# High and low parts of the hidden state as one moving operand of 512 columns in the first sweep over the experts

## The chip, the cores and the metric

The kernel runs on one core of a Trainium2 chip. The metric is the time of the whole program on the device, in microseconds, as the median of several runs. A change within 0.2% of it is about what a measurement of this kernel cannot tell from no change.

## The reference, cut to what matters

The program computes two transformer layers with a mixture of experts and then a third block, whose last part is this one (256 tokens, width 1024):

```
sc = einsum('bshcd,hckd->bshck', q, sub_keys)         # 8 heads x 2 sides x 128 keys
v1, i1 = top_k(sc[..., 0, :], 16);  v2, i2 = top_k(sc[..., 1, :], 16)
cand = v1[..., :, None] + v2[..., None, :]            # 16 x 16 pairs per head
top, pos = top_k(cand, 16);  idx = i1 * 128 + i2 at pos;  gate = softmax(top)
u   = expert_down[idx];  act  = gelu(einsum('bld,blhkd->blhk', h, u))
coef = gate * act
out = einsum('blhk,blhkd->bld', coef, expert_up[idx]) # added to the residual
```

There are 128 x 128 = 16384 experts, each a row of 1024 numbers in `expert_down` and one in `expert_up`. All arithmetic is float32.

## The kernel before, in words

The kernel is a chain of stages; each has its own program for every engine, and a barrier stands between two. The last part is peer_scores (scores of keys), peer_values, peer_grid (gates laid out over the experts) and peer_mix (second sweep, over `expert_up`). The change is in the first sweep, `peer_values`, and in where its operands lie.

The sweep computes the Gelu of h times **every** expert row, in 128 units of 128 experts, and does the search for the best keys and pairs beside it. The matrix engine takes float32 operands rounded to a format called fp32r, so each product of a and b is made of three: with a = high + low, high(a) high(b) + high(a) low(b) + low(a) high(b). For h the two parts are made once (`peer_scores`, L2573 and L2583). For a unit n of expert rows (512 KB, loaded into slot n % 6):

- **high(n)**, L2638, ScalarE: the rounded copy, 128 x 1024, into slot n % 3.
- **low(n)**, L2664, VectorE: row minus rounded row, written over the loaded row.
- **product(n)**, L2616, TensorE: eight blocks of 128 of the contraction, three matmuls each with 256 tokens as moving columns, all into one half of a PSUM bank, n % 3 (banks 0 to 2). The weights are a block of the rows, high twice and low once.
- **Gelu(n)**, L2653, ScalarE: from PSUM into the column block n of `pair_grid`.

Order by engine. ScalarE: high(0), high(1), high(2), and then for every n: wait for product(n), high(n+3), Gelu(n). VectorE: for every n low(n), then a piece of side work: for n below 40, four units of five have a **row search** (`rows`, `top16`: five operations on 128 scores, each waiting for the one before it); from 41 to 72 every second unit has a **pair search** (`pairs`: an addition and the same five on 256); 73 and 74 have `lift` and `places`; unit 76 has `norm`, which waits for ScalarE's Exp in unit 74 (`EXP_AT`); from 77 to 100 every second has one of **mark, take and gather** (one operation on 2048 each). TensorE: product(n) waits for low(n) and for Gelu(n-3), whose bank it takes; before unit 102 (`TURN_AT`) come six transposes, whose results ScalarE copies out in three (L2647 to L2649). SyncE loads unit n+6 when product(n) is done.

All waits are semaphores that count up: `high_made`, `low_made`, `summed` (a product is done), `gelued`, and so on.

Of the kernel before, what the change touches and what calls it, by code (L numbers as in the profile page):

```python
# [15 lines left out]
F32 = mybir.dt.float32  # L16
U32 = mybir.dt.uint32
I32 = mybir.dt.int32
F32R = mybir.dt.float32r
# [4 lines left out]
P = 128  # L24
T = 256
# [223 lines left out]
def half(ps, b):  # L249

    return ps[:, b // 2, (b % 2) * T:(b % 2) * T + T]
# [2224 lines left out]
class PeerMemory:  # L2476
# [3 lines left out]
    def __init__(self, k, ctx):  # L2480
        self.k = k
        grid_at = -(-k.nc.sbuf_base // 32) * 32
        self.qt = k.nc.alloc_sbuf_tensor_at("peer_q", [P, 2 * PH, T], F32, offset=grid_at + 48 * 1024)
        linear(k, "peer_queries", [("peer_query", 4, 0)], k.h, self.qt, ahead=0)
        self.grid = k.sb("pair_grid", [P, NK, T], ctx=ctx)
        self.lists = k.sb("peer_lists", [P, 2, T], ctx=ctx)
        self.i2_minus = k.sb("peer_second_list", [P, T], F32R, ctx=ctx)
        self.ident, self.ones, self.iota = (k.sb(f"peer_{n}", [P, P], F32R, ctx=ctx) for n in ("ident", "ones", "iota"))

        def units(name, first, n, dt, shape=None):  # L2490
            return k.nc.alloc_sbuf_tensor_at(name, shape or [P, n, D], dt, offset=k.ring_at + first * 4096)
        self.raw = units("expert_rows", 0, PEER_RAW, F32)
        self.low = units("expert_rows_low", 0, PEER_RAW, F32R)
        self.high = units("expert_rows_high", PEER_RAW, PEER_HIGH, F32R)
        self.h_high = units("peer_h_high", PEER_RAW + PEER_HIGH, 2, F32R, [P, KC, T])
        self.h_low = k.nc.alloc_sbuf_tensor_at("peer_h_low", [P, KC, T], F32R, offset=k.h_at)
        self.first = units("peer_first", PEER_RAW, 2, F32, [P, 4, QUAD, NK])
        self.second = units("peer_second", PEER_RAW + 2, 2, F32, [P, 4, QUAD, NK])
        self.apart = units("peer_apart", PEER_RAW + 4, 2, F32, [P, 4, QUAD * NK])
        self.coef_high = units("peer_coef_high", PEER_RAW + PEER_HIGH, 1, F32R, [P, 4, T])  # L2500
        self.coef_low = units("peer_coef_low", PEER_RAW + PEER_HIGH + 1, 1, F32R, [P, 4, T])
        self.rows = k.nc.alloc_sbuf_tensor_at("out_rows", [P, TT, D], F32, offset=k.h_at)

        self.at = grid_at + 64 * 1024
        self.kn = self.place("peer_keys", [P, 2 * PH, P])
        self.kt = self.place("peer_keysT", [P, 2 * PH, NK])
        self.sc = self.place("peer_scores", [P, TT, 2 * PH, NK])
        self.at = grid_at + 104 * 1024
        self.v = self.place("peer_best", [P, TT, 2 * PH, TOPK])
        self.ix = self.place("peer_best_ix", [P, TT, 2 * PH, TOPK], U32)  # L2510
        self.ixf = self.place("peer_best_ixf", [P, TT, 2 * PH, TOPK])
        self.top = self.place("peer_top", [P, TT, PH, TOPK])
        self.pos = self.place("peer_pos", [P, TT, PH, TOPK], U32)
        self.pa = self.place("peer_pos_a", [P, TT, PH, TOPK], U32)
        self.pf = self.place("peer_pos_f", [P, 2, TT, PH, TOPK])
        self.key = self.place("peer_key", [P, 2, TT, PH, TOPK])
        self.stat = self.place("peer_stat", [P, TT, PH])
        self.cand = self.place("peer_cand", [P, 2, TOPK, TOPK])
        self.hot = self.place("peer_hot", [P, PH, TOPK, TOPK])
        assert self.at <= grid_at + 128 * 1024  # L2520
# [17 lines left out]
def peer_scores(k, m):  # L2538

    H = PH  # L2540
    qt, kn, kt, sc = m.qt, m.kn, m.kt, m.sc
    with k.stage("peer_scores") as st:
        block = st.block
        in_keys, turned, moved, scored, scores_out, h_made, h_split = st.signals(7)

        @block.gpsimd
        def _(pool):
            st.clear_last(pool)

        @block.sync  # L2550
        def _(sp):
            sp.dma_start(kn[:], k.a["peer_sub_keys_2"][0].rearrange("h c k d -> k (h c) d")).then_inc(in_keys, 16)
            for n in range(PEER_RAW):
                m.load(sp, n)

        def four(b):
            return k.ps[:, b:b + 4, :].rearrange("p b (e t) -> p (b e) t", e=4)

        @block.tensor
        def _(pe):  # L2560
            pe.wait_ge(in_keys, 16)
            for n in range(2 * H):
                mm = pe.transpose(four(0)[:, n], kn[:, n], k.ident)
            mm.then_inc(turned, 1)
            pe.wait_ge(moved, 1)
            for i in range(TT):
                for n in range(2 * H):
                    mm = pe.matmul(four(4 * (1 - i))[:, n], qt[:, n, i * P:(i + 1) * P], kt[:, n], start=True, stop=True)
                mm.then_inc(scored, 1)

        @block.scalar
        def _(act):
            act.activation(m.h_high[:], k.h, ACT.Copy).then_inc(h_made, 1)  # L2573
            act.wait_ge(turned, 1)
            act.activation(kt[:], four(0), ACT.Copy).then_inc(moved, 1)
            for i in range(TT):
                act.wait_ge(scored, i + 1)
                act.activation(sc[:, i], four(4 * (1 - i)), ACT.Copy).then_inc(scores_out, 1)

        @block.vector  # L2580
        def _(dve):
            dve.wait_ge(h_made, 1)
            dve.tensor_tensor(m.h_low[:], k.h, m.h_high[:].bitcast(F32), ALU.subtract).then_inc(h_split, 1)  # L2583
            for dst, src in ((m.ident, k.ident), (m.ones, k.ones), (m.iota, k.iota)):
                dve.tensor_copy(dst[:], src).then_inc(h_split, 1)


def peer_values(k, m):
# [5 lines left out]
    SCORES_END, LATE = 96 - 16, 104  # L2594
    with k.stage("peer_values") as st:
        block = st.block
        high_made, low_made, summed, gelued, chain, ranked, apart, exped, normed, chosen, turned, moved = st.signals(12)

        @block.gpsimd
        def _(pool):  # L2600
# [8 lines left out]
        def product(pe, s, it):  # L2609
            n = it * PEER_RAW + s  # L2610
            pe.wait_ge(low_made, n + 1)
            pe.wait_ge(gelued, n + 1)
            for c in range(KC):
                hi, lo = m.high[:, s % PEER_HIGH, c * P:(c + 1) * P], m.low[:, s, c * P:(c + 1) * P]
                for q, (w, x) in enumerate(((hi, m.h_high), (hi, m.h_low), (lo, m.h_high))):
                    mm = pe.matmul(half(k.ps, 2 * (s % 3)), w, x[:, c], start=(c == 0 and q == 0), stop=(c == KC - 1 and q == 2))  # L2616
            mm.then_inc(summed, 1)

        @block.tensor
# [11 lines left out]

        @block.scalar
        def _(act):
            act.sem_inc(gelued, 3)

            def high(n):
                act.wait_ge(k.experts_in[n % PEER_RAW], loaded_units(n))
                act.activation(m.high[:, n % PEER_HIGH], m.raw[:, n % PEER_RAW], ACT.Copy).then_inc(high_made, 1)  # L2638

            for n in range(PEER_HIGH):  # L2640
                high(n)
            for n in range(NK):
                if n == SCORES_END:
                    act.wait_ge(ranked, 1)
                if n == TURN_AT:
                    act.wait_ge(turned, 1)
                    act.activation(m.lists[:, 0], half(k.ps, 8), ACT.Copy).then_inc(moved, 1)  # L2647
                    act.activation(m.lists[:, 1], half(k.ps, 10), ACT.Copy).then_inc(moved, 1)
                    act.activation(m.i2_minus[:], half(k.ps, 9), ACT.Copy, scale=-1.0).then_inc(moved, 1)  # L2649
                act.wait_ge(summed, n + 1)  # L2650
                if n + PEER_HIGH < NK:
                    high(n + PEER_HIGH)
                act.activation(m.grid[:, n:n + 1], half(k.ps, 2 * (n % 3)).unsqueeze(1), ACT.Gelu).then_inc(gelued, 1)  # L2653
                if n == EXP_AT:
                    act.wait_ge(apart, 1)
                    act.activation(top[:], top[:], ACT.Exp).then_inc(exped, 1)

        @block.vector
        def _(dve):
# [54 lines left out]
            def gather(n):  # L2714
                side, i = divmod(n, TT)
                dve.tensor_reduce(key[:, side, i].rearrange("p h r -> p (h r)"), f, AX.X, ALU.add).then_inc(chosen, 1)

            for n in range(NK):
                low(n)
                if n < 40 and n % 5 < 4:  # L2720
                    rows(n // 5 * 4 + n % 5)
                if n == 40:
# [5 lines left out]
                    lift()  # L2728
                if n == 74:
                    places()  # L2730
                if n == EXP_AT + 2:
                    norm()
                if 77 <= n < 101:
                    if (n - 77) % 6 == 0:
# [2 lines left out]
                        take((n - 77) // 6)  # L2737
                    if (n - 77) % 6 == 4:
                        gather((n - 77) // 6)


def peer_grid(k, m):
# [337 lines left out]
```

## Time and profile before

| | us |
|---|---|
| median of 3 runs | 4452.86 |
| lowest and highest run | 4451.96, 4454.59 |
| the profiled execution, whole | 4446.22 |
| its span in the profile | 4444.4 |
| TensorE busy in the span | 3906.9 (88%) |
| VectorE busy | 2328.8 (52%) |
| ScalarE busy | 1864.2 (42%) |

The profiled execution is one of its own, 6.64 us below the median of the three; 1.82 us of it lie outside the span. PE is TensorE's matmul, PEld its weight load, DVE VectorE, ACT ScalarE. The stage peer_values lies at 3499.3 to 3873.0 us of the span. In the timeline a matmul's record is longer than the distance to the next one's start: matmuls overlap, and what one costs in a row of them is read from the starts.

### The profile page before, as it was taken

Reading aid. Unit: us, or ns where it says so; the run is one execution under the profiler, and the core shown is the slowest. Engines: PE = TensorE matmul, PEld = TensorE weight load, DVE = VectorE, ACT = ScalarE, POOL = GpSimd, SP = SyncE. Lnnn points to the kernel's source line nnn. Section 1 sums busy time; section 2 is a strip of 40 time slices with the busy share of each in tenths; the row PEclk is TensorE's granted clock in tenths of the full one; section 3 lists DMA queues with packets and bytes.
Section 4 is the critical chain, followed back from the end, with each engine's and each line's share of the span. In section 5 each row is a group of like instructions: output and inputs, shape, how many; then the busy total and the mean of one; then the engine's idle time right before and its main releaser. Section 6 shows DMA issues by size and latency. Waiting matters only on the chain. (4 is left out here: it accounts for less than half of the span.)

```text
span 4444.4 us, 55601 instructions
## 1 busy us (share of the span) xinstructions
PE 3906.9 (88%) x21753; PEld 3255.8 (73%) x21753; DVE 2328.8 (52%) x2807; ACT 1864.2 (42%) x1955; POOL 54.5 (1%) x28
## 2 busy tenths in 40 slices
PE   6899878997948778999999996795687899999999
PEld 1792867997938656777777875795366899977887
DVE  0332632443346226888888872334423588455665
ACT  0333151333341416767767662343221344433554
POOL 0000000000000000000000000000000000000000
PEclk9999878998969779999999998897578999956999
DMA  7456003443500117999999982352003456501665
GB/s 237 160 190 227 5 1 114 170 151 133 190 23 1 38 57 265 361 363 361 363 363 361 363 317 85 114 183 74 6 15 119 127 184 180 161 1 35 193 193 165
DMA packets 308099, 738.78 MB, mean 166 GB/s; under 512 B 16154, under 2 KB 16609, under 8 KB 307937
## 3 DMA queue, kind: packets, MB, share of 16 engines
q1 hardware_dynamic: 307936, 736.60, 48.2%
q8 instruction: 105, 1.72, 0.2%
q14 instruction: 58, 0.47, 0.0%
HBM read 735.50 MB, written 1.05 MB: 166 GB/s over the span
## 5 line engine op out<-in xcount | busy, mean ns | idle before, releaser
L1777 DVE TENSOR_TENSOR weight_ring_low<-weight_ring,weights_high 128x2048 fp32r<-128x2048 f32 x336 | 772.8, 2341 | 148.9 <-ACT weights_high L1723 148.9
L1723 ACT ACTIVATE weights_high<-weight_ring 128x2048 fp32r<-128x2048 f32 x336 | 618.3, 1908 | 6.6 <-DMA weight_ring<-in_moe_w 6.6
L305 PE MATMUL psum_all<-h_high_projections,high_projections 128*128 128x256 f32 x1536 | 436.5, 284 | 50.0 <-DVE weight_ring_low L341 50.0
L305 PE MATMUL psum_all<-h_low_projections,high_projections 128*128 128x256 f32 x1536 | 436.2, 284 | 0.0
L305 PE MATMUL psum_all<-h_high_projections,weight_ring_low 128*128 128x256 f32 x1536 | 430.6, 280 | 0.0
L1665 PE MATMUL psum_all<-weights_high,expert_in_turn_high 128*128 128x512 f32 x896 | 359.3, 401 | 17.5 <-DVE weight_ring_low L1777 11.4
L341 DVE TENSOR_TENSOR weight_ring_low<-weight_ring,high_projections 128x2048 fp32r<-128x2048 f32 x96 | 215.4, 2288 | 303.3 <-ACT high_projections L327 303.3
L1665 PE MATMUL psum_all<-weights_high,expert_in_turn_low 128*128 128x512 f32 x896 | 356.2, 398 | 0.0
L1665 PE MATMUL psum_all<-weight_ring_low,expert_in_turn_high 128*128 128x512 f32 x896 | 351.7, 393 | 0.0
L305 PEld LDWEIGHTS psum_all<-h_high_projections,high_projections 128*128 128x128 f32 x1536 | 291.9, 190 | 51.2 <-issue 51.2
L305 PEld LDWEIGHTS psum_all<-h_high_projections,weight_ring_low 128*128 128x128 f32 x1536 | 296.1, 193 | 0.0
L2616 PE MATMUL psum_all<-peer_h_high,expert_rows_high 128*128 128x256 f32 x1024 | 291.1, 284 | 5.0 <-DVE expert_rows_low L2664 5.0
L305 PEld LDWEIGHTS psum_all<-h_low_projections,high_projections 128*128 128x128 f32 x1536 | 292.2, 190 | 0.0
L2616 PE MATMUL psum_all<-peer_h_low,expert_rows_high 128*128 128x256 f32 x1024 | 290.6, 284 | 0.0
L2616 PE MATMUL psum_all<-peer_h_high,expert_rows_low 128*128 128x256 f32 x1024 | 290.6, 284 | 0.0
L2638 ACT ACTIVATE expert_rows_high<-expert_rows 128x1024 fp32r<-128x1024 f32 x128 | 135.2, 1058 | 192.8 <-PE psum_all L2616 190.7
L1665 PEld LDWEIGHTS psum_all<-weights_high,expert_in_turn_high 128*128 128x128 f32 x896 | 168.7, 188 | 61.5 <-issue 20.5
L2664 DVE TENSOR_TENSOR expert_rows_low<-expert_rows,expert_rows_high 128x1024 fp32r<-128x1024 f32 x128 | 156.6, 1225 | 96.8 <-ACT expert_rows_high L2638 94.8
L2616 PEld LDWEIGHTS psum_all<-peer_h_high,expert_rows_high 128*128 128x128 f32 x1024 | 197.5, 193 | 5.4 <-DVE expert_rows_low L2664 5.4
L1665 PEld LDWEIGHTS psum_all<-weight_ring_low,expert_in_turn_high 128*128 128x128 f32 x896 | 168.4, 188 | 40.2
L2616 PEld LDWEIGHTS psum_all<-peer_h_low,expert_rows_high 128*128 128x128 f32 x1024 | 197.5, 193 | 0.0
L2616 PEld LDWEIGHTS psum_all<-peer_h_high,expert_rows_low 128*128 128x128 f32 x1024 | 197.4, 193 | 0.0
(563 smaller groups left out, 7811.7 us busy)
## 6 DMA issues: line engine op xcount, KB each, us to landing
weight_ring<-in_moe_w SPq DMA_DIRECT2D x336, 1024.0 KB, 5.2
weight_ring<-in_w_in SPq DMA_DIRECT2D x48, 2048.0 KB, 8.5
expert_rows<-in_peer_down SPq DMA_DIRECT2D x128, 512.0 KB, 3.6
expert_rows<-in_peer_up SPq DMA_DIRECT2D x128, 512.0 KB, 3.6
weight_ring<-in_ada_w SPq DMA_DIRECT2D x24, 2048.0 KB, 8.0
weight_ring<-in_ffn_w SPq DMA_DIRECT2D x21, 2048.0 KB, 7.8
weight_ring<-in_w_out SPq DMA_DIRECT2D x6, 2048.0 KB, 8.1
weight_ring<-in_w_up_dn SPq DMA_DIRECT2D x4, 2048.0 KB, 8.0
```

The lines of the kernel that those rows point to most:

```text
L305: mm = pe.matmul(half(k.ps, 4 * (g % R) + j), w[:, c, j * P:(j + 1) * P], x[:, c], start=(c == 0 and n == 0), stop=(c == KC - 1 and n == 2))
L341: dve.tensor_tensor(k.low[:, g % R, part], k.ring[:, g % R, part], high[:, i % H, part].bitcast(F32), ALU.subtract).then_inc(low_made, 1)
L1665: mm = pe.matmul(k.ps[:, q, :], x[:, c], w[:, c], start=(c == 0 and n == 0), stop=(c == KC - 1 and n == 2))
L1723: act.activation(high[:, q, h * HALF:(h + 1) * HALF], k.ring[:, q, h * HALF:(h + 1) * HALF], ACT.Copy).then_inc(high_made[q], 1)
L1777: dve.tensor_tensor(k.low[:, q, part], k.ring[:, q, part], high[:, q, part].bitcast(F32), ALU.subtract).then_inc(low_made[q], 1)
L2616: mm = pe.matmul(half(k.ps, 2 * (s % 3)), w, x[:, c], start=(c == 0 and q == 0), stop=(c == KC - 1 and q == 2))
L2638: act.activation(m.high[:, n % PEER_HIGH], m.raw[:, n % PEER_RAW], ACT.Copy).then_inc(high_made, 1)
L2664: dve.tensor_tensor(m.low[:, n % PEER_RAW], m.raw[:, n % PEER_RAW], m.high[:, n % PEER_HIGH].bitcast(F32), ALU.subtract).then_inc(low_made, 1)
```

## The change

In `peer_scores` and the memory plan, the two parts of h stand side by side in one tensor `peer_h_both` with two halves; `h_high` and `h_low` are views of it. A ring of four tiles `peer_value_sums` (128 x 256 each) is new.

In `product` the block `hi` is loaded once with a moving operand of 512 columns (high and low part of h), which fills a whole PSUM bank: columns 0 to 255 get high x high, 256 to 511 high x low. The block `lo` with 256 columns of h's high part is added to columns 0 to 255. So the two halves must be added outside of TensorE:

- ScalarE, **copy(n)**: columns 256 to 511 from PSUM into the ring, before high(n+3); it waits for product(n), and for Gelu(n-4).
- VectorE, **join(n)**: ring tile plus columns 0 to 255 from PSUM, into the ring; it stands after low(n+3) and waits for copy(n).
- ScalarE, Gelu(n) reads the ring tile and now waits for join(n).
- TensorE: product(n) waits for join(n-3) in place of Gelu(n-3).

`norm` moves from unit 76 to unit 82.

```diff
--- before.py
+++ after.py
@@ -2492,8 +2492,10 @@
         self.raw = units("expert_rows", 0, PEER_RAW, F32)
         self.low = units("expert_rows_low", 0, PEER_RAW, F32R)
         self.high = units("expert_rows_high", PEER_RAW, PEER_HIGH, F32R)
-        self.h_high = units("peer_h_high", PEER_RAW + PEER_HIGH, 2, F32R, [P, KC, T])
-        self.h_low = k.nc.alloc_sbuf_tensor_at("peer_h_low", [P, KC, T], F32R, offset=k.h_at)
+        both_at = k.ring_at + (PEER_RAW + PEER_HIGH) * 4096
+        self.h_both = k.nc.alloc_sbuf_tensor_at("peer_h_both", [P, 2, (k.h_at - both_at) // 4], F32R, offset=both_at)
+        self.h_high, self.h_low = (self.h_both[:, e, 0:KC * T].rearrange("p (c t) -> p c t", c=KC) for e in range(2))
+        self.sums = units("peer_value_sums", PEER_RAW + PEER_HIGH + 2, 1, F32, [P, 4, T])
         self.first = units("peer_first", PEER_RAW, 2, F32, [P, 4, QUAD, NK])
         self.second = units("peer_second", PEER_RAW + 2, 2, F32, [P, 4, QUAD, NK])
         self.apart = units("peer_apart", PEER_RAW + 4, 2, F32, [P, 4, QUAD * NK])
@@ -2570,7 +2572,7 @@
 
         @block.scalar
         def _(act):
-            act.activation(m.h_high[:], k.h, ACT.Copy).then_inc(h_made, 1)
+            act.activation(m.h_high, k.h, ACT.Copy).then_inc(h_made, 1)
             act.wait_ge(turned, 1)
             act.activation(kt[:], four(0), ACT.Copy).then_inc(moved, 1)
             for i in range(TT):
@@ -2580,7 +2582,7 @@
         @block.vector
         def _(dve):
             dve.wait_ge(h_made, 1)
-            dve.tensor_tensor(m.h_low[:], k.h, m.h_high[:].bitcast(F32), ALU.subtract).then_inc(h_split, 1)
+            dve.tensor_tensor(m.h_low, k.h, m.h_high.bitcast(F32), ALU.subtract).then_inc(h_split, 1)
             for dst, src in ((m.ident, k.ident), (m.ones, k.ones), (m.iota, k.iota)):
                 dve.tensor_copy(dst[:], src).then_inc(h_split, 1)
 
@@ -2594,7 +2596,7 @@
     SCORES_END, LATE = 96 - 16, 104
     with k.stage("peer_values") as st:
         block = st.block
-        high_made, low_made, summed, gelued, chain, ranked, apart, exped, normed, chosen, turned, moved = st.signals(12)
+        high_made, low_made, summed, gelued, chain, ranked, apart, exped, normed, chosen, turned, moved, joined, copied = st.signals(14)
 
         @block.gpsimd
         def _(pool):
@@ -2609,11 +2611,13 @@
         def product(pe, s, it):
             n = it * PEER_RAW + s
             pe.wait_ge(low_made, n + 1)
-            pe.wait_ge(gelued, n + 1)
+            pe.wait_ge(joined, n + 1)
+            out = k.ps[:, s % 3, :]
             for c in range(KC):
                 hi, lo = m.high[:, s % PEER_HIGH, c * P:(c + 1) * P], m.low[:, s, c * P:(c + 1) * P]
-                for q, (w, x) in enumerate(((hi, m.h_high), (hi, m.h_low), (lo, m.h_high))):
-                    mm = pe.matmul(half(k.ps, 2 * (s % 3)), w, x[:, c], start=(c == 0 and q == 0), stop=(c == KC - 1 and q == 2))
+                pe.matmul(out.rearrange("p (e t) -> p e t", e=2), hi, m.h_both[:, :, c * T:(c + 1) * T], start=(c == 0), stop=False,
+                          skip_group_check=True)
+                mm = pe.matmul(out[:, 0:T], lo, m.h_high[:, c], start=False, stop=(c == KC - 1), skip_group_check=True)
             mm.then_inc(summed, 1)
 
         @block.tensor
@@ -2631,7 +2635,7 @@
 
         @block.scalar
         def _(act):
-            act.sem_inc(gelued, 3)
+            act.sem_inc(joined, 3)
 
             def high(n):
                 act.wait_ge(k.experts_in[n % PEER_RAW], loaded_units(n))
@@ -2648,9 +2652,13 @@
                     act.activation(m.lists[:, 1], half(k.ps, 10), ACT.Copy).then_inc(moved, 1)
                     act.activation(m.i2_minus[:], half(k.ps, 9), ACT.Copy, scale=-1.0).then_inc(moved, 1)
                 act.wait_ge(summed, n + 1)
+                if n >= 4:
+                    act.wait_ge(gelued, n - 3)
+                act.activation(m.sums[:, n % 4], k.ps[:, n % 3, T:2 * T], ACT.Copy).then_inc(copied, 1)
                 if n + PEER_HIGH < NK:
                     high(n + PEER_HIGH)
-                act.activation(m.grid[:, n:n + 1], half(k.ps, 2 * (n % 3)).unsqueeze(1), ACT.Gelu).then_inc(gelued, 1)
+                act.wait_ge(joined, n + 4)
+                act.activation(m.grid[:, n:n + 1], m.sums[:, n % 4:n % 4 + 1], ACT.Gelu).then_inc(gelued, 1)
                 if n == EXP_AT:
                     act.wait_ge(apart, 1)
                     act.activation(top[:], top[:], ACT.Exp).then_inc(exped, 1)
@@ -2715,8 +2723,14 @@
                 side, i = divmod(n, TT)
                 dve.tensor_reduce(key[:, side, i].rearrange("p h r -> p (h r)"), f, AX.X, ALU.add).then_inc(chosen, 1)
 
+            def join(n):
+                dve.wait_ge(copied, n + 1)
+                dve.tensor_tensor(m.sums[:, n % 4], m.sums[:, n % 4], k.ps[:, n % 3, 0:T], ALU.add).then_inc(joined, 1)
+
             for n in range(NK):
                 low(n)
+                if n >= PEER_HIGH:
+                    join(n - PEER_HIGH)
                 if n < 40 and n % 5 < 4:
                     rows(n // 5 * 4 + n % 5)
                 if n == 40:
@@ -2728,7 +2742,7 @@
                     lift()
                 if n == 74:
                     places()
-                if n == EXP_AT + 2:
+                if n == EXP_AT + 8:
                     norm()
                 if 77 <= n < 101:
                     if (n - 77) % 6 == 0:
@@ -2737,6 +2751,8 @@
                         take((n - 77) // 6)
                     if (n - 77) % 6 == 4:
                         gather((n - 77) // 6)
+            for n in range(NK - PEER_HIGH, NK):
+                join(n)
 
 
 def peer_grid(k, m):
```

What moves on ScalarE, in the middle of the row searches. In the names `expert_rows_in0` to 5 are the loads; `stage0_signal2` is `summed`, 3 `gelued`, 12 `joined`. Before:

```order
875 L2653 ACTIVATE pair_grid<-psum_all 128x256
876 L2638 ACTIVATE expert_rows_high<-expert_rows 128x1024 [waits expert_rows_in2,stage0_signal2]
877 L2653 ACTIVATE pair_grid<-psum_all 128x256
878 L2638 ACTIVATE expert_rows_high<-expert_rows 128x1024 [waits expert_rows_in3,stage0_signal2]
879 L2653 ACTIVATE pair_grid<-psum_all 128x256
```

And after:

```order
877 L2661 ACTIVATE pair_grid<-peer_value_sums 128x256 [waits stage0_signal12]
878 L2657 ACTIVATE peer_value_sums<-psum_all 128x256 [waits stage0_signal3,stage0_signal2]
879 L2642 ACTIVATE expert_rows_high<-expert_rows 128x1024 [waits expert_rows_in1]
880 L2661 ACTIVATE pair_grid<-peer_value_sums 128x256 [waits stage0_signal12]
881 L2657 ACTIVATE peer_value_sums<-psum_all 128x256 [waits stage0_signal3,stage0_signal2]
```

The copy stands ahead of high and takes over its wait for the product; the Gelu behind high has a wait of its own, for the join.

What moves on VectorE, in the same stretch; `stage0_signal0` is `high_made`, 4 the chain of the searches, 13 `copied`. Before:

```order
1088 L2664 TENSOR_TENSOR expert_rows_low<-expert_rows,expert_rows_high 128x1024 [waits stage0_signal0]
1089 L2668 MAX peer_best<-peer_scores 128x8
1090 L2669 MAX_INDEX peer_best_ix<-peer_best,peer_scores 128x8 [waits stage0_signal4]
1091 L2670 MATCH_REPLACE peer_scores<-peer_best,peer_scores 128x128 [waits stage0_signal4]
1092 L2671 MAX peer_best<-peer_scores 128x8 [waits stage0_signal4]
1093 L2672 MAX_INDEX peer_best_ix<-peer_best,peer_scores 128x8 [waits stage0_signal4]
```

And after:

```order
1088 L2672 TENSOR_TENSOR expert_rows_low<-expert_rows,expert_rows_high 128x1024 [waits stage0_signal0,stage0_signal4]
1089 L2728 TENSOR_TENSOR peer_value_sums<-peer_value_sums,psum_all 128x256 [waits stage0_signal13]
1090 L2672 TENSOR_TENSOR expert_rows_low<-expert_rows,expert_rows_high 128x1024 [waits stage0_signal0]
1091 L2728 TENSOR_TENSOR peer_value_sums<-peer_value_sums,psum_all 128x256 [waits stage0_signal13]
1092 L2676 MAX peer_best<-peer_scores 128x8
1093 L2677 MAX_INDEX peer_best_ix<-peer_best,peer_scores 128x8 [waits stage0_signal4]
```

A join stands between every low and the side work of its unit.

## Rows read from the trace of the kernel before

**Rows 1.** Windows: start:end, us, busy (x instructions) of PE, PEld, DVE, ACT, POOL, clock, DMA, GB/s.
```profile
3617.40:3720.10 102.70, 102.70 (x858) 102.70 (x857) 87.35 (x186) 47.91 (x72) 0.00 (x0) 1.00 0.60 182
...
3793.40:3873.00 79.60, 79.19 (x661) 78.98 (x659) 30.90 (x26) 35.24 (x56) 0.00 (x0) 1.00 0.61 182
```

**Rows 2.** Waits, 3499 to 3873 us: who waited for whom, total us, times, longest.
```profile
ACT expert_rows_high L2638 <- PE psum_all L2616: 190.7, 121, 4.5
...
PE psum_all L2616 <- DVE expert_rows_low L2664: 5.0, 2, 4.6
```

**Rows 3.** Lines' instructions: ns shortest/median/longest, first and last start in us.
```profile
L2664 DVE TENSOR_TENSOR expert_rows_low<-expert_rows,expert_rows_high x128: 1215/1226/1228, 3499.3 to 3865.1; 128x1024 fp32r<-128x1024 f32 x128
...
L2653 ACT ACTIVATE pair_grid<-psum_all x128: 363/367/388, 3508.0 to 3872.6; 128x256 f32<-128x256 f32 x128
...
L1526 DVE TENSOR_TENSOR ffn_hidden<-ffn_silu,psum_all x28: 409/412/422, 783.5 to 979.9; 128x256 f32<-128x256 f32 x28
```

**Rows 4.** Timeline, TensorE: start, us, instruction; products at half and full clock.
```profile
3503.97 0.41 PE L2616 MATMUL psum_all<-peer_h_high,expert_rows_high 128*128 128x256 f32 x1
3504.19 0.41 PE L2616 MATMUL psum_all<-peer_h_low,expert_rows_high 128*128 128x256 f32 x1
...
3559.81 0.28 PE L2616 MATMUL psum_all<-peer_h_high,expert_rows_high 128*128 128x256 f32 x1
3559.93 0.28 PE L2616 MATMUL psum_all<-peer_h_low,expert_rows_high 128*128 128x256 f32 x1
```

**Rows 5.** Timeline, TensorE in peer_mix: matmuls of 512 columns, two a row.
```profile
4200.66 0.61 PE L2866 MATMUL psum_all<-expert_rows_low,peer_coef_high 128*128 128x512 f32 x2
4201.11 0.62 PE L2866 MATMUL psum_all<-expert_rows_high,peer_coef_low 128*128 128x512 f32 x2
```

**Rows 6.** Timeline, ScalarE, a unit; in brackets idle before and releaser.
```profile
3655.41 1.06 ACT L2638 ACTIVATE expert_rows_high<-expert_rows 128x1024 fp32r<-128x1024 f32 x1 [1.55 <-PE psum_all L2616]
3656.38 0.37 ACT L2653 ACTIVATE pair_grid<-psum_all 128x256 f32<-128x256 f32 x1
```

**Rows 7.** Timeline, VectorE, the same unit, a pair search; the next low.
```profile
3656.51 1.23 DVE L2664 TENSOR_TENSOR expert_rows_low<-expert_rows,expert_rows_high 128x1024 fp32r<-128x1024 f32 x1 [0.43 <-ACT expert_rows_high L2638]
3657.65 0.42 DVE L2681 TENSOR_TENSOR peer_cand<-peer_best 128x256 f32<-128x256 f32 x1
...
3660.61 1.23 DVE L2664 TENSOR_TENSOR expert_rows_low<-expert_rows,expert_rows_high 128x1024 fp32r<-128x1024 f32 x1
```

**Rows 8.** Timeline, ScalarE, the Exp of unit 74 and the high behind it.
```profile
3720.12 1.28 ACT L2656 ACT_TABLE_LOAD   x1
3721.42 0.42 ACT L2656 ACTIVATE peer_top<-peer_top 128x256 f32<-128x256 f32 x1
3721.74 1.04 ACT L2638 ACTIVATE expert_rows_high<-expert_rows 128x1024 fp32r<-128x1024 f32 x1
```

**Rows 9.** Timeline, ScalarE, two of the three list copies in unit 102.
```profile
3798.33 0.38 ACT L2647 ACTIVATE peer_lists<-psum_all 128x256 f32<-128x256 f32 x1
3798.60 0.39 ACT L2648 ACTIVATE peer_lists<-psum_all 128x256 f32<-128x256 f32 x1
```

**Rows 10.** Timeline, VectorE: a row search from its start to next low; low(3).
```profile
3500.47 0.29 DVE L2668 MAX8 peer_best<-peer_scores 128x8 f32<-128x128 f32 x1
...
3502.31 1.23 DVE L2664 TENSOR_TENSOR expert_rows_low<-expert_rows,expert_rows_high 128x1024 fp32r<-128x1024 f32 x1
...
3508.26 1.22 DVE L2664 TENSOR_TENSOR expert_rows_low<-expert_rows,expert_rows_high 128x1024 fp32r<-128x1024 f32 x1
```

**Rows 11.** Timeline, VectorE: a take and the next low.
```profile
3728.68 2.29 DVE L2712 TENSOR_TENSOR peer_hot<-peer_hot,peer_best_ixf 128x2048 f32<-128x2048 f32 x1
3731.00 1.23 DVE L2664 TENSOR_TENSOR expert_rows_low<-expert_rows,expert_rows_high 128x1024 fp32r<-128x1024 f32 x1
```

**Rows 12.** Windows of two other stretches, both with waits of TensorE.
```profile
1700.00:1720.00 20.00, 17.62 (x78) 13.81 (x77) 17.16 (x10) 14.31 (x10) 0.00 (x0) 1.00 0.87 315
...
780.00:800.00 20.00, 15.58 (x121) 15.38 (x121) 15.15 (x14) 10.66 (x10) 0.00 (x0) 0.91 0.34 110
```

## The prediction

> **What bounds the kernel now.** I read the busy slices first, then one table over the stage that the change touches, then its waits, then the timeline of single units. The page has TensorE busy for 88% of the span. The stage peer_values runs from 3499.3 [rows 3] to 3873.0 us, 373.7 us for 128 units of expert rows. Among the pair searches TensorE is filled for all of 102.70 us at clock 1.00, VectorE is busy for 85% of them and ScalarE for 47%; at the end TensorE is as full and VectorE has 39% [rows 1]. The waits say the same: ScalarE waits 190.7 us for TensorE's sums, TensorE only 5.0 us for VectorE [rows 2]. So the stage goes at TensorE's pace. The first start of "low" is at 3499.3 us and the last, 127 units on, at 3865.1 [rows 3]: 2.88 us a unit.
>
> **What TensorE saves.** A unit has 24 matmuls of 256 columns, which start 0.12 us apart [rows 4]: 24 x 0.12 = 2.88 us, as found. The busy column's 284 ns is not what one costs, since they overlap. A matmul of 512 columns starts 0.226 us after the one before it (two in 0.45 us) [rows 5]. After the change a unit has 8 of 512 and 8 of 256: 8 x (0.226 + 0.12) = 2.77 us. The columns stay the same, 768 for each of the eight blocks; only the 0.013 us or so beside each removed matmul goes. The most that can be won is 128 x 0.11 = 14 us. No row has a moving operand in two pieces of 256 apart in SBUF; 0.12 (second piece free) and 0.24 (nothing saved) are the ends for it, and I take 0.226. It matters only if TensorE stays the bound.
>
> The Trainium skill ("TensorE: Matmul & The Clock Gate", Back-to-back issue gap) has a matmul cost its columns at 2.4 GHz plus some 2.5 ns. By that the merge would save 8 x 2.5 ns = 0.02 us a unit, 2.6 us in all; the rows show 0.12 us where it has 0.109, so I go by the rows.
>
> **What is added.** Per unit ScalarE gets a copy of 256 columns from PSUM to SBUF, VectorE an addition of 256 columns with one operand in PSUM (join), and the order gets new waits. In ScalarE's order the sequence of a unit is copy(n), high(n+3), then Gelu(n), and the Gelu waits for join(n). In VectorE's order join(n) stands behind low(n+3), and low(n+3) waits for high(n+3). Before, Gelu(n) waited for TensorE alone. Both engines work in order, so a circle closes in every unit:
>
> high(n+3) on ScalarE, low(n+3) and join(n) on VectorE, Gelu(n), copy(n+1), high(n+4) on ScalarE.
>
> Nothing in it can run ahead: behind the waiting Gelu(n) stand copy(n+1) and high(n+4), for which low(n+4), join(n+1) and with it product n+4 wait. The period of the circle, piece by piece:
> - high 1.06, from its end to the start of low 0.04 (3655.41 + 1.06 to 3656.51) [rows 6, 7];
> - from the start of low to the next on VectorE 1.14 (3656.51 to 3657.65) [rows 7];
> - join 0.41: a multiplication of 256 columns with one operand in PSUM, in the dense feed-forward stage, took that [rows 3]; then again 0.04 across engines;
> - Gelu, now with its input in SBUF: the Exp of the same size between SBUF tiles took 0.42 and the next started 0.32 after it [rows 8];
> - copy: 0.38 for the same copy; less 0.10 of overlap with the next, as after Exp, 0.28 [rows 8, 9].
>
> TensorE is not in the circle: product n+3 is released by join(n) and low(n+3), and its sum is asked for by copy(n+3), about two periods after join(n), when its 2.77 us are over. The other new wait, of copy(n) for Gelu(n-4), is met by ScalarE's own order.
>
> Sum: 1.06 + 0.04 + 1.14 + 0.41 + 0.04 + 0.32 + 0.28 = 3.29 us, more than the 2.77 of TensorE. Bounds: with no overlap at all on an engine 1.06 + 0.04 + 1.23 + 0.41 + 0.04 + 0.42 + 0.38 = 3.58; with start-to-start distances throughout (high 0.97 [rows 6], join 0.33, Gelu and copy 0.27 [rows 9]) and signals free, 2.98. I take 3.29, since it adds a full duration only where the other engine follows.
>
> VectorE's side work makes some units longer still, because it follows join in the order and the next low comes behind it. Join costs 0.33 there (0.41 less 0.08, as 1.23 of low less 1.14).
> - units with a row search: 1.14 + 0.33 + 1.84 (3500.47 to 3502.31 [rows 10]) = 3.31; 29 from unit 3 on;
> - units with a pair search: 1.14 + 0.33 + 2.96 (3657.65 to 3660.61 [rows 7]) = 4.43; 16 of them;
> - units with mark, take or gather: 1.14 + 0.33 + 2.32 (3728.68 to 3731.00 [rows 11]) = 3.79; 12 of them;
> - the other 67 units from 3 to 126: 3.29.
>
> Before, a unit without side work made good what a long one lost, as the 0.43 us of idle VectorE before a low among the pairs shows [rows 7]. In the circle it does not: a light unit costs 3.29 however little VectorE has to do.
>
> **The sum.** 29 x 3.31 + 16 x 4.43 + 12 x 3.79 + 67 x 3.29 = 432.8 us. The Exp in unit 74 now stands in the circle: from its table load to the next high 1.62 us [rows 8]; the load for the Gelu after it hides behind low and join. The three list copies in unit 102 add 3 x 0.27 = 0.8 [rows 9]. Together 435.2, against 3508.26 to 3865.1 = 356.8 us now [rows 3, 10]: +78.4. At the start the copy before high(3) adds 0.3. At the end the last Gelu ends 7.9 us after the start of the last low (3872.6 + 0.37 [rows 3]); then TensorE, no longer behind, starts product 127 at 1.55 us after it (low 1.14, join 0.41), ends at about 4.5, and copy, join and Gelu take it to 5.8: -2.1. In all +76.6 us. The move of norm from unit 76 to 82 costs nothing: its three short operations fall into a light unit, in which VectorE has 3.29 - 1.14 - 0.33 = 1.8 us beside low and join; a whole row search needs 1.84. Where h's parts lie costs nothing: the same two operations write them, before the stage. The DMAs are issued by the end of a product as before, and each has longer units to land in. No later stage reads anything other than before.
>
> 4446.2 us of the profiled execution + 76.6 = 4522.8. The median of the runs is 4452.9, 6.6 above the profiled one, so 4529 is what I predict of it.
>
> The Trainium skill ("VectorE: DVE Perf Modes", The TRN2 errata) says that operations of both engines that read SBUF pay a latency that is exposed between instructions. By that the circle would be the 3.58 of the upper end. The rows have the next ScalarE operation start 0.1 us before the record of the last one ends.
>
> **Rivals.**
> - *Latencies laid end to end.* The circle is there, but with the full durations: light units 3.58, row units 3.58 also. 67 x 0.29 + 29 x 0.27 = +27: 4556. For it: no row shows a join behind a low. Against it: the overlap in all rows. 6%.
> - *Only VectorE's throughput binds*, the four-deep ring of sums giving the slack. Row stretch 29 x 3.31 + 8 x 1.47 = 107.8 for 106.6 now; pairs 16 x (4.43 + 1.47) = 94.4 for 92.2; then TensorE's 2.77 for 2.88 in the last 55 units, -6: about 4450, no change. For it: VectorE's 85%. Against it: the ring holds sums, but the order of the instructions does not use it. 5%.
> - *TensorE stays the bound*, all side work hidden: -14, 4439. It decides only if Gelu(n) did not hold up high(n+4), which the order denies. 3%.
> - *The clock falls.* TensorE would idle 0.5 us in 3.29, up to 1.7 in 4.43. At the lower level (1.2 GHz), as at 3504 us, 256-column matmuls started 0.21 apart [rows 4]: 8 x (0.43 + 0.21) = 5.1 us a unit, and the product becomes the bound: 124 x 5.1 - 356.8 = +276, 4729. For it: a stretch of 20 us in which TensorE was filled for 15.58 had 0.91. Against it: one in which it was filled for 17.62 kept 1.00 [rows 12]. 4%.
>
> **How the numbers follow.** The forecast has 82%; its own bounds, 2.98 and 3.58 for light units, give 67 x -0.31 = -21 and +27, so 4508 to 4556. The range is 4508 to 4558; it leaves out the faster cases, no change, the fallen clock and a little of the forecast. A change within 0.2% (9 us) is about what a measurement cannot tell from none. Slower: 82 + 6 + 4 = 92%; same: 5%; faster: 3%.
>
> **What would show it.** Right: the stage takes about 450 us; low starts 3.3 us apart at its end, and alternately 4.4 and 3.3 among the pairs; ScalarE waits in Gelu for VectorE's join some 1.6 us a unit, VectorE before low for ScalarE about as long in light units; TensorE's waits are for join, some 0.5 us a unit, and the clock stays at 1.00. Wrong: TensorE without waits in the light units at the end, or ScalarE's waits still for TensorE. A granted clock of 0.5 in mid-stage would be the last rival.

## The result, and the profile after

| | before | after |
|---|---|---|
| median, us | 4452.41 (4 runs) | 4521.19 (4 runs, 4515.62 to 4527.67) |
| the profiled execution, us | 4446.22 | 4523.53 |
| its span, us | 4444.4 | 4521.7 |

The changed kernel takes 1.0156 times as long, 95% interval 1.0138 to 1.0173: slower, by some 69 us of the median. The forecast for the median was 4529. The spans of the two profiled executions differ by 77.3 us; the forecast for that was 76.6. Three executions of the experiments below ran at a much lower granted clock (4772.99 us of the kernel before, 6596.61 with join ahead of low, 4789.6 with the extra copy beside the circle) and are left out of all medians and ratios.

First the starts of low and of join in the changed kernel (columns as in [rows 3]); L2672 answers to L2664 there.

```profile
L2672 DVE TENSOR_TENSOR expert_rows_low<-expert_rows,expert_rows_high x128: 1216/1226/1228, 3499.5 to 3942.0; 128x1024 fp32r<-128x1024 f32 x128
...
L2728 DVE TENSOR_TENSOR peer_value_sums<-peer_value_sums,psum_all x128: 412/415/423, 3509.6 to 3947.3; 128x256 f32<-128x256 f32 x128
```

A low is as long as before, but from the first to the last one 442.5 us pass in place of 365.8, which is 76.7 more. A join takes 0.415 us, as the 0.41 taken from another stage. Now two windows, the stretch with the pair searches and the end of the stage (columns as in [rows 1]).

```profile
3620.40:3746.90 126.50, 102.44 (x542) 82.28 (x542) 95.95 (x223) 55.07 (x101) 0.00 (x0) 1.00 0.46 141
3865.00:3945.00 80.00, 73.81 (x391) 59.23 (x390) 37.80 (x49) 40.56 (x77) 0.00 (x0) 1.00 0.51 159
```

No engine is filled: TensorE 81% and 92% of the time, VectorE 76% and 47%, ScalarE 44% and 51%. The granted clock stays at 1.00, the upper level. Waits of the changed kernel, as [rows 2]:

```profile
ACT pair_grid L2661 <- DVE peer_value_sums L2728: 230.1, 128, 2.8
DVE expert_rows_low L2672 <- ACT expert_rows_high L2642: 133.8, 69, 20.6
PEld psum_all L2618 <- DVE expert_rows_low L2672: 96.0, 122, 4.8
PE psum_all L2618 <- DVE peer_value_sums L2728: 56.1, 121, 2.0
```

ScalarE waits for VectorE and VectorE for ScalarE; TensorE waits for both operations of VectorE, its weight load for low and its first matmul for join. Before, ScalarE waited for TensorE (190.7 us), VectorE for ScalarE (94.8 us) and TensorE hardly at all, so no two engines waited for each other. One turn at the end of the stage, first VectorE and then ScalarE in the timeline (as [rows 7] and [rows 6] for the kernel before):

```profile
3922.47 1.23 DVE L2672 TENSOR_TENSOR expert_rows_low<-expert_rows,expert_rows_high 128x1024 fp32r<-128x1024 f32 x1 [1.70 <-ACT expert_rows_high L2642]
3923.62 0.41 DVE L2728 TENSOR_TENSOR peer_value_sums<-peer_value_sums,psum_all 128x256 f32<-128x256 f32 x1
3925.74 1.23 DVE L2672 TENSOR_TENSOR expert_rows_low<-expert_rows,expert_rows_high 128x1024 fp32r<-128x1024 f32 x1 [1.71 <-ACT expert_rows_high L2642]
```

```profile
3924.07 0.42 ACT L2661 ACTIVATE pair_grid<-peer_value_sums 128x256 f32<-128x256 f32 x1 [1.62 <-DVE peer_value_sums L2728]
3924.39 0.37 ACT L2657 ACTIVATE peer_value_sums<-psum_all 128x256 f32<-128x256 f32 x1
3924.65 1.05 ACT L2642 ACTIVATE expert_rows_high<-expert_rows 128x1024 fp32r<-128x1024 f32 x1
```

Read it as a relay: low starts at 3922.47, join at 3923.62 and ends at 3924.03; Gelu starts at 3924.07, copy at 3924.39, high at 3924.65 and ends at 3925.70; low starts again at 3925.74. That is 3.27 us, and in no moment of it do ScalarE and VectorE both work. The idle time before low (1.70) is ScalarE's part of the turn, that before Gelu (1.62) VectorE's.

### The profile page after: what moved, and what is told of

The parts are those of the page before. It is cut to its first block and busy times, and to the rows that moved or that the text cites. A ratio compares the mean times of both kernels' runs of the same rounds, so it can differ in the third digit from the quotient of the medians.

```text
span 4521.7 us, 53808 instructions
## 1 busy us (share of the span) xinstructions
PE 3927.3 (87%) x20729; PEld 3199.6 (71%) x20729; DVE 2372.3 (52%) x2935; ACT 1904.4 (42%) x2083; POOL 54.5 (1%) x28
## 3 DMA queue, kind: packets, MB, share of 16 engines
HBM read 735.50 MB, written 1.05 MB: 163 GB/s over the span
## 5 line engine op out<-in xcount | busy, mean ns | idle before, releaser
L305 PE MATMUL psum_all<-h_high_projections,weight_ring_low 128*128 128x256 f32 x1536 | 433.4, 282 | 0.0
L2618 PE MATMUL psum_all<-peer_h_both,expert_rows_high 128*128 128x512 f32 x1024 | 374.9, 406 | 60.8 <-DVE peer_value_sums L2728 56.1
L2618 PEld LDWEIGHTS psum_all<-peer_h_both,expert_rows_high 128*128 128x128 f32 x1024 | 192.8, 188 | 136.9 <-DVE expert_rows_low L2672 96.0
L2620 PE MATMUL psum_all<-peer_h_both,expert_rows_low 128*128 128x256 f32 x1024 | 286.9, 280 | 0.0
L2672 DVE TENSOR_TENSOR expert_rows_low<-expert_rows,expert_rows_high 128x1024 fp32r<-128x1024 f32 x128 | 156.8, 1225 | 136.6 <-ACT expert_rows_high L2642 133.8
L318 ACT ACTIVATE projected<-psum_all 128x1024 f32<-128x1024 f32 x48 | 49.3, 1027 | 352.3 <-PE psum_all L305 352.3
L1665 PEld LDWEIGHTS psum_all<-weights_high,expert_in_turn_low 128*128 128x128 f32 x896 | 168.7, 188 | 36.2
L2620 PEld LDWEIGHTS psum_all<-peer_h_both,expert_rows_low 128*128 128x128 f32 x1024 | 193.9, 189 | 0.0
L2918 DVE TENSOR_TENSOR expert_rows_low<-expert_rows,expert_rows_high 128x1024 fp32r<-128x1024 f32 x128 | 156.8, 1225 | 66.1 <-ACT expert_rows_high L2895 66.1
```

The source lines that it names most:

```text
L305: mm = pe.matmul(half(k.ps, 4 * (g % R) + j), w[:, c, j * P:(j + 1) * P], x[:, c], start=(c == 0 and n == 0), stop=(c == KC - 1 and n == 2))
L318: act.activation(dest[:, blk:blk + 4], src, ACT.Copy).then_inc(copied, 1)
L1665: mm = pe.matmul(k.ps[:, q, :], x[:, c], w[:, c], start=(c == 0 and n == 0), stop=(c == KC - 1 and n == 2))
L2618: pe.matmul(out.rearrange("p (e t) -> p e t", e=2), hi, m.h_both[:, :, c * T:(c + 1) * T], start=(c == 0), stop=False, skip_group_check=True)
L2620: mm = pe.matmul(out[:, 0:T], lo, m.h_high[:, c], start=False, stop=(c == KC - 1), skip_group_check=True)
L2672: dve.tensor_tensor(m.low[:, n % PEER_RAW], m.raw[:, n % PEER_RAW], m.high[:, n % PEER_HIGH].bitcast(F32), ALU.subtract).then_inc(low_made, 1)
```

## The experiments

Each kernel is timed against the kernel before on the same chip (medians there 4447.4, 4446.7 and 4446.9 us). The changed kernel is compared with them by its ratio, 1.0156. The ratios and intervals are as recorded; the quotient of two medians can differ from them by 0.0004.

| kernel | median, us | ratio to before, 95% |
|---|---|---|
| Gelu one unit later | 4447.50 | 1.0004 (0.9994 to 1.0013) |
| join ahead of low | 4452.36 | 1.0014 (1.0005 to 1.0022) |
| an extra copy on the circle | 4550.29 | 1.0233 (1.0214 to 1.0252) |
| an extra copy beside it | 4521.84 | 1.0168 (1.0145 to 1.0190) |
| the wide product alone | 4432.69 | 0.9972 (0.9963 to 0.9981) |
| Gelu later, side work spread | 4437.30 | 0.9977 (0.9967 to 0.9987) |
| side work spread, circle closed | 4516.45 | 1.0161 (1.0144 to 1.0178) |

**Cut the circle on ScalarE.** The copy and the join stay, only the place of the Gelu differs.

```diff
-                act.wait_ge(joined, n + 4)
-                act.activation(m.grid[:, n:n + 1], m.sums[:, n % 4:n % 4 + 1], ACT.Gelu).then_inc(gelued, 1)
+                if n > 0:
+                    gelu(n - 1)                      # the same two lines, for unit n - 1
...
+            gelu(NK - 1)
```

> The changed kernel, but ScalarE's order in a unit is copy(n), high(n+3), Gelu(n-1) in place of Gelu(n). Theory (circle): Gelu(n-1) finds join(n-1) long done, so high(n+4) no longer hangs on join(n). Then VectorE's throughput binds where it has side work (29 x 3.31 + 8 x 1.47 = 107.8 us in the row stretch, 16 x 5.90 = 94.4 in the pair stretch) and TensorE's 2.76 us a unit elsewhere (some 152 us for 55 units): 355 us from low(3) to low(127) against 431.6 in the changed kernel as it is, near the 356.8 of the kernel before; about 4450 us, ratio to before 0.998 to 1.003. ScalarE's 230 us of waits for join go to nearly none. Rival 1 (what VectorE and ScalarE have to do in all is too much, whatever the order): the operations are the same, so about 4521, ratio 1.0156. Rival 2 (the wide matmul with its operand in two pieces is slower than its parts): TensorE binds at more than 2.88 us a unit, ratio over 1.005.

Ratio 1.0004: the whole loss is gone, with every operation still there. From low(3) to low(127) it takes 354.9 us (355 expected; 356.8 in the kernel before, 433.6 in the changed kernel). Its ScalarE in the light units (those without side work) at the end, in the timeline:

```profile
3840.87 0.38 ACT L2661 ACTIVATE peer_value_sums<-psum_all 128x256 f32<-128x256 f32 x1 [1.19 <-PE psum_all L2620]
3841.15 1.06 ACT L2642 ACTIVATE expert_rows_high<-expert_rows 128x1024 fp32r<-128x1024 f32 x1
3842.10 0.41 ACT L2646 ACTIVATE pair_grid<-peer_value_sums 128x256 f32<-128x256 f32 x1
3843.70 0.38 ACT L2661 ACTIVATE peer_value_sums<-psum_all 128x256 f32<-128x256 f32 x1 [1.20 <-PE psum_all L2620]
```

The Gelu follows high without a wait, and ScalarE waits for TensorE again; the period is 2.83 us. Where VectorE has much side work, Gelu still waits for join (49 times, 50.3 us in all, not 230.1, but more than the "nearly none" expected). There VectorE is the bound: it is filled for 94.27 of 99 us in the row stretch and 77.21 of 80 in the pair stretch, and from 3508 to 3712 us its trace shows no wait at all, while both other engines wait for it:

```profile
3501.00:3600.00 99.00, 97.54 (x541) 83.00 (x540) 94.27 (x283) 56.34 (x98) 0.00 (x0) 0.99 0.58 174
3620.00:3700.00 80.00, 79.42 (x439) 66.86 (x438) 77.21 (x176) 44.65 (x82) 0.00 (x0) 1.00 0.60 182
```

**Cut it on VectorE.**

```diff
             for n in range(NK):
-                low(n)
                 if n >= PEER_HIGH:
                     join(n - PEER_HIGH)
+                low(n)
```

> The changed kernel, but on VectorE join(n-3) stands ahead of low(n) in place of behind it; ScalarE's order is untouched, Gelu(n) still waits for join(n). Theory (circle): join(n) no longer waits for high(n+3), which can run beside it, so the circle is cut at another place. What is left is join, Gelu, copy, high: 0.41 + 0.04 + 0.32 + 0.27 + 1.06 + 0.04 and low 1.14 in parallel to part of it, under 2.8 us. About 4450, ratio to before 0.998 to 1.006 (a long pair search can hold up join, and so Gelu and high, a little). Rival 1 (sum of work): 4521, ratio 1.0156. A third possibility, that the wait of Gelu for join alone does the harm wherever join stands: between, 1.008 to 1.015.

Ratio 1.0014. Gelu(n) waits for join(n) as in the changed kernel, so the third possibility, that this wait alone does the harm, falls: it is the wait together with the place of join behind low. In the trace it is a little worse than the cut on ScalarE, 363.6 us from low(3) to low(127) for 354.9, though the two ratios can hardly be told apart. A pair search now holds up join, Gelu, copy and high in turn, and the light unit behind it takes 1.79 us where it took 1.47. The Gelu behind such a search:

```profile
3653.14 0.42 ACT L2661 ACTIVATE pair_grid<-peer_value_sums 128x256 f32<-128x256 f32 x1 [3.06 <-DVE peer_value_sums L2728]
```

**One more operation, on the circle and beside it.** The same copy of 128x256 in both, from a tile that the stage does not write to one that nobody reads. The diff shows both places; each kernel has one of them, with the line on `extra` ahead of it.

```diff
+                act.wait_ge(extra, n)
+                act.activation(m.scratch[:], k.xT[:, 0], ACT.Copy).then_inc(extra, 1)    # beside: here
                 act.wait_ge(joined, n + 4)
                 act.activation(m.grid[:, n:n + 1], m.sums[:, n % 4:n % 4 + 1], ACT.Gelu).then_inc(gelued, 1)
+                act.wait_ge(extra, n)
+                act.activation(m.scratch[:], k.xT[:, 0], ACT.Copy).then_inc(extra, 1)    # on the circle: here
```

> The changed kernel with one more ScalarE copy of 128x256 from SBUF to an unused tile in every unit, right behind Gelu(n), so on the circle; nothing else. Theory (circle): light units 3.26 + 0.32 = 3.58, 67 x 0.32 = 21 us; row units 3.31 to 3.58, 29 x 0.27 = 8 us; nothing in pair and mark units, where VectorE's side work is longer than Gelu, copy, high and this: +29 us on the changed kernel, about 4550, ratio to before 1.022. Rival (ScalarE has room: busy 42%): +0, ratio 1.0156.

> The same extra ScalarE copy in every unit, but ahead of Gelu's wait for join, between high(n+3) and Gelu(n), where ScalarE idles 1.6 us. Theory (circle): beside the circle, which runs over VectorE then, so no cost: ratio to before as the changed kernel's, 1.0156, and 0.0065 below that of the copy behind Gelu. Rival (ScalarE's total work or its contention with VectorE makes the period): the same as behind Gelu, whatever that is.

On the circle it costs 0.0065 of ratio against beside it, some 28 us of the median, and beside it nothing that can be told (1.0168 with an interval that holds 1.0156). The traces say it more sharply: from low(3) to low(127) 463.0 us with the copy on the circle, 433.4 with it beside and 433.6 without it. Both ScalarE timelines at the end of the stage, first on the circle, then beside:

```profile
3940.38 0.42 ACT L2662 ACTIVATE pair_grid<-peer_value_sums 128x256 f32<-128x256 f32 x1 [1.62 <-DVE peer_value_sums L2731]
3940.70 0.40 ACT L2664 ACTIVATE peer_scratch<-residual 128x256 f32<-128x256 f32 x1
...
3943.94 0.42 ACT L2662 ACTIVATE pair_grid<-peer_value_sums 128x256 f32<-128x256 f32 x1 [1.62 <-DVE peer_value_sums L2731]
```

```profile
3932.17 0.42 ACT L2664 ACTIVATE pair_grid<-peer_value_sums 128x256 f32<-128x256 f32 x1 [1.32 <-DVE peer_value_sums L2731]
...
3933.70 0.41 ACT L2662 ACTIVATE peer_scratch<-residual 128x256 f32<-128x256 f32 x1
3935.43 0.42 ACT L2664 ACTIVATE pair_grid<-peer_value_sums 128x256 f32<-128x256 f32 x1 [1.32 <-DVE peer_value_sums L2731]
```

On the circle the period is 3.56 us and the wait for join is still 1.62; beside it the wait shrinks to 1.32 and the period stays at 3.26. The same engine has room for the same work in one place and none in the other.

**The wide product alone.** Copy and join are gone, so this kernel leaves columns 256 to 511, the product of high(row) and low(h), out of the sum.

```diff
-            pe.wait_ge(joined, n + 1)
+            pe.wait_ge(gelued, n + 1)
...
-                act.activation(m.sums[:, n % 4], k.ps[:, n % 3, T:2 * T], ACT.Copy).then_inc(copied, 1)
...
-                act.activation(m.grid[:, n:n + 1], m.sums[:, n % 4:n % 4 + 1], ACT.Gelu).then_inc(gelued, 1)
+                act.activation(m.grid[:, n:n + 1], k.ps[:, n % 3, 0:T].unsqueeze(1), ACT.Gelu).then_inc(gelued, 1)
...
-                    join(n - PEER_HIGH)
```

> The wide product alone: TensorE's matmuls as in the changed kernel (8 of 512 and 8 of 256 columns a unit), but the copy and join are gone, Gelu reads columns 0 to 255 straight from PSUM and, as in the kernel before, gates the bank. It leaves the product of high(row) and low(h) out of the sum. Theory: all side work is hidden as before and TensorE binds at 2.76 us a unit for 2.88: 124 x 0.12 = 14 to 15 us less, about 4433 beside 4447.7, ratio 0.9968. By the sentence on some 2.5 ns a matmul in the Trainium skill (TensorE: Matmul & The Clock Gate, Back-to-back issue gap) the gain would be near nothing: 0.9995. Rival (the second weight load was what cost, and a pair of 512 and 256 shares it): more than 20 us, under 0.9955.

Ratio 0.9972. From the first to the last low 352.0 us pass for 365.8, 2.77 us a unit. Its TensorE in the timeline:

```profile
3839.88 0.39 PE L2618 MATMUL psum_all<-peer_h_both,expert_rows_high 128*128 128x512 f32 x1
3840.11 0.28 PE L2620 MATMUL psum_all<-peer_h_both,expert_rows_low 128*128 128x256 f32 x1
3840.22 0.39 PE L2618 MATMUL psum_all<-peer_h_both,expert_rows_high 128*128 128x512 f32 x1
```

A pair of 512 and 256 columns takes 0.34 to 0.35 us (0.23 and 0.11), with the operand in two pieces. That is what the merge of the matmuls is worth here, 14 us of 4447: the columns are the same, and only a little beside each removed matmul goes. Both other values of the expectation, 0.9995 and under 0.9955, lie outside the interval.

**Spread VectorE's side work, with the Gelu later.** The three lists name the units with a row search, with a pair search, and with mark, take or gather. The small tiles of the search trade places, so that those still in use after unit 102 lie where the results of units from 112 on go.

```diff
-EXP_AT = 74
+EXP_AT = 84
+ROWS = [1, 2, 3, 5, 6, 7, 9, 10, 12, 13, 15, 16, 17, 19, 20, 22, 23, 24, 26, 27, 29, 30, 32, 33, 34, 36, 37, 39, 40, 41, 43, 44]
+PAIRS = [47, 49, 51, 54, 56, 58, 61, 63, 66, 68, 70, 73, 75, 77, 80, 82]
+BIG = [86, 87, 89, 92, 94, 95, 97, 99, 101, 102, 104, 106]
...
-    TURN_AT = 17 * PEER_RAW
+    TURN_AT = 18 * PEER_RAW
```

> The kernel with Gelu one unit later, and VectorE's side work spread: row searches in 32 of units 1 to 44, pair searches in 16 of 47 to 82, Exp in 84, mark, take and gather in 12 of 86 to 106, so that no stretch asks more of VectorE than TensorE's pace gives; the transposes go from unit 102 to 108, for which six small tiles change places. Theory: with the circle cut, VectorE's throughput binds in the row stretch (107.7 us for 37 units with the Gelu later) and the pair stretch (96.4 for 33); VectorE's whole load to unit 107 is 108 x 1.47 + some 138 us = 297 us, for which TensorE needs 108 x 2.76 = 298. So TensorE binds nearly all through: 343 to 347 us from low(3) to low(127) for 354.8, ratio to before 0.9975 to 0.9985. Rival (something other than VectorE's stretches holds the Gelu-later kernel at before's time): ratio 1.000 still. A load so near to the pace could also lose some in stalls: then between the two.

Ratio 0.9977: faster than the kernel before and the changed one, and within the interval of the wide product alone, though all of copy and join is there. From low(3) to low(127) it takes 347.6 us, just above the 343 to 347 expected. Over 330 us VectorE is busy for 90% and TensorE is full:

```profile
3520.00:3850.00 330.00, 330.00 (x1890) 288.29 (x1889) 296.50 (x627) 201.04 (x360) 0.00 (x0) 1.00 0.60 187
```

**The spreading without the cut.** As the last one, but `gelu(n)` in place of `gelu(n - 1)`.

> The kernel with spread side work, but with Gelu(n) back in its place in unit n, as in the changed kernel: the circle is closed again. Theory (circle): a unit costs the greater of 3.26 us and VectorE's own 3.31, 4.43 or 3.79, wherever the side work stands; from low(3) to low(127) 29 to 31 row units, 16 pair units, 12 others with side work, the rest 3.26: 430 us as in the changed kernel, less nothing for the spreading. About 4521, ratio to before 1.0155 to 1.017. Rival (the spreading, and not the place of Gelu, brought the gain): near 0.998, or at least well under 1.010.

Ratio 1.0161, and 433.3 us from low(3) to low(127), as in the changed kernel (433.6; 430 expected). Spreading the side work gains nothing while the circle is closed; at the end low starts every 3.26 us, with VectorE idle for 1.70 before it, as in the changed kernel:

```profile
3928.83 1.23 DVE L2678 TENSOR_TENSOR expert_rows_low<-expert_rows,expert_rows_high 128x1024 fp32r<-128x1024 f32 x1 [1.70 <-ACT expert_rows_high L2645]
...
3932.09 1.23 DVE L2678 TENSOR_TENSOR expert_rows_low<-expert_rows,expert_rows_high 128x1024 fp32r<-128x1024 f32 x1 [1.70 <-ACT expert_rows_high L2645]
```

## Why the prediction was right

**The circle's period.** Forecast 3.29 us, found 3.26 to 3.27. The terms: high 1.05 (forecast 1.06), the step to low 0.04 (0.04), low to join 1.14 to 1.15 (1.14), join 0.41 (0.41), the step to Gelu 0.04 (0.04), Gelu to copy 0.32 (0.32), copy to high 0.26 (0.28). Nothing was off by more than 0.02: the copy took 0.37 where I had 0.38, and high started 0.11 before its end where I had 0.10.

**The stretches.** Starts of low in the changed kernel, units 40, 73 and 101; unit 3 starts at 3508.45 and unit 127 at 3942.0.

```profile
3631.47 1.23 DVE L2672 TENSOR_TENSOR expert_rows_low<-expert_rows,expert_rows_high 128x1024 fp32r<-128x1024 f32 x1 [1.70 <-ACT expert_rows_high L2642]
...
3757.97 1.22 DVE L2672 TENSOR_TENSOR expert_rows_low<-expert_rows,expert_rows_high 128x1024 fp32r<-128x1024 f32 x1 [1.70 <-ACT expert_rows_high L2642]
...
3856.46 1.23 DVE L2672 TENSOR_TENSOR expert_rows_low<-expert_rows,expert_rows_high 128x1024 fp32r<-128x1024 f32 x1 [1.70 <-ACT expert_rows_high L2642]
```

| units | by the forecast's terms | found |
|---|---|---|
| 3 to 39 | 29 x 3.31 + 8 x 3.29 = 122.3 | 123.0 |
| 40 to 72 | 16 x 4.43 + 17 x 3.29 = 126.8 | 126.5 |
| 73 to 100 | 12 x 3.79 + 16 x 3.29 + 1.6 = 99.7 | 98.5 |
| 101 to 126 | 26 x 3.29 + 0.8 = 86.3 | 85.6 |

Together 433.6 for 435.2. In the first row the units with a row search took 3.33 us each, not 3.31. In the third row the forecast has 1.2 us too many: 16 light units took 0.03 less each, the four gathers 3.67 and not the 3.79 of a take, and the Exp with its table load added 1.3 and not 1.6.

**The two ends.** The last Gelu ends 6.1 us after the start of the last low (3947.71 + 0.42 less 3942.04), forecast 5.8. The copy ahead of high(3) cost nothing; forecast 0.3.

**The sum, and what was luck.** From the first low to the end of the last Gelu the stage takes 448.6 us where it took 373.7: +75.0, forecast +76.6. The rest of the 77.3 lies outside the stage, mostly behind it, where the forecast had nothing: 573.6 us from that Gelu to the end of the span, and 571.4 before. Over the traces of all nine kernels this time runs from 568.3 to 573.6, though none of them changes an operation there, so I take it for scatter. That 76.6 and 77.3 differ by 0.7 is luck in part; the 1.6 us in the stage is the measure of the forecast.

**The median.** It was forecast at 4529 and came at 4521.19, inside the range. The step that was 8 us too high is the last addition: I took the median to lie 6.6 us above the profiled execution, as before. In the changed kernel the profiled execution, 4523.53, lies 2.3 us above the median. Where one execution lies among its like is chance, and 6.6 should not have been carried over.

**TensorE's saving.** Forecast 14 us if it stayed the bound; the wide product alone gave a ratio of 0.9972, and the moving operand in two pieces costs what the neighbouring row said. In the changed kernel the saving is idle time: between two products TensorE waits for join (56.1 us in 121 units, 0.46 each, forecast some 0.5), and its weight load, which goes first, for low (96.0 us). I had named only join.

**Rivals.** *Latencies laid end to end* would give a period of 3.58; it is 3.26. *VectorE's throughput* was the rival with the right prices for another kernel: it gave 107.8 and 94.4 us for the row and the pair stretch, and the kernel with the Gelu later shows 107.7 and 96.4 (units 3 to 39 and 40 to 72; unit 40 alone, with its copy of the key numbers, takes 1.92, which the 94.4 left out). There it is the next bound, and the spread then removes it. *TensorE as the bound* of the whole sweep is seen only with the join gone, or with the circle cut and the work spread. *The clock* did not fall: 1.00 in both windows above, with TensorE filled for 81% of the first.

The trace does not agree with the sentence on an exposed SBUF latency ("VectorE: DVE Perf Modes", The TRN2 errata, in the Trainium skill): in the changed kernel too the next operation of ScalarE starts 0.10 us before the end of the record of the last, and the circle is 3.26, not the 3.58 without overlap.

## What to carry to other kernels

When a result must pass through a second engine, look at where its consumer stands in the first engine's order: a wait right behind the operation that feeds the second engine closes a circle, and the period is then the sum of both engines' parts, however idle each looks. Walk the two orders once around before you add up busy times; and put the consumer one turn later, if the ring of tiles has room. Merging matmuls over the same columns saved some 0.01 us here for each one that went, so it pays only if what it adds on the other engines is kept off the bound: 0.9977 with the circle cut and the side work spread, 1.0156 without.

## What I had not expected of the hardware

With the Gelu one unit later TensorE's pace in the light units at the end is 2.83 us, not the 2.77 of the product alone, though the trace shows no wait of TensorE there. With the side work spread as well it is 2.77 again. The starts of the same matmul, eight pairs (one unit's worth) apart, first with the Gelu later, then with the spread:

```profile
3839.61 0.40 PE L2618 MATMUL psum_all<-peer_h_both,expert_rows_high 128*128 128x512 f32 x1
...
3842.44 0.40 PE L2618 MATMUL psum_all<-peer_h_both,expert_rows_high 128*128 128x512 f32 x1
```

```profile
3839.85 0.39 PE L2621 MATMUL psum_all<-peer_h_both,expert_rows_high 128*128 128x512 f32 x1
...
3842.62 0.39 PE L2621 MATMUL psum_all<-peer_h_both,expert_rows_high 128*128 128x512 f32 x1
```

The 0.06 us is not one gap between two units: every pair of 512 and 256 columns takes 0.35 to 0.36 us in the first and 0.34 to 0.35 in the second. With join ahead of low the pace is 2.83 too. The order of the instructions in these units is the same in the first two kernels, and what slows the pairs stays open; it is some 1.5 us over the last 26 units.
